# Tile loads and ScalarE copies moved ahead in the first two heads of a query, key, value stage

## The reference

```
def diff_attention(h, positions, w_qkv, lq1, lk1, lq2, lk2, subln_g, w_o, lambda_init):
    q, k, v = jnp.split(h @ w_qkv, 3, axis=-1)
    ...
    q = apply_rotary(q, cos, sin) * (HEAD_DIM ** -0.5)
    k = apply_rotary(k, cos, sin)
    ...
        s = jnp.einsum('bqhcd,bkhcd->bhcqk', q_blk, k, preferred_element_type=jnp.float32)
        p = jax.nn.softmax(s, axis=-1)
        a = p[:, :, 0] - lam * p[:, :, 1]
        return jnp.einsum('bhqk,bkhe->bqhe', a.astype(v.dtype), v)
```

## Time and profile before

| what | value |
|---|---|
| median of 3 runs | 2399.89 us (2398.41 to 2400.56) |
| the profiled execution, its own time | 2399.84 us |
| its span, first to last instruction | 2398.0 us |
| mean granted TensorE clock | 0.989 of 2.4 GHz |
| TensorE busy | 2311.8 us, 96% of the span |
| VectorE, ScalarE, GpSimd busy | 58%, 41%, 47% |

### The profile page before, as it was taken

One profiled execution on the slowest core, in us unless ns is written; L12 is line 12 of the kernel. 1 busy time (PEld: TensorE's weight loads), 2 busy tenths in 40 slices (PEclk: granted clock), 3 DMA queues, 4 the chain that ended last, 5 costly groups with the idle time before them and its releaser, 6 DMA issues.

```text
span 2398.0 us, 26048 instructions
## 1 busy us (share of the span) xinstructions
PE 2311.8 (96%) x10260; PEld 1884.2 (79%) x10260; DVE 1401.9 (58%) x1311; ACT 991.5 (41%) x1116; POOL 1138.8 (47%) x711
## 2 busy tenths in 40 slices
PE   8899989999999999999999999998999999999997
PEld 6688767777777888888888778887778888888886
DVE  7566799999375555556423654445565555563223
ACT  5112168888444444444312443233444444442112
POOL 1112113333467777775122677752776677732221
PEclk9999999999999999999999999999999999999998
DMA  3553374451322222322522322224222222234222
GB/s 130 170 175 120 132 201 114 97 135 36 124 93 80 79 79 80 93 84 99 200 91 90 108 71 74 75 88 175 80 88 82 86 79 79 83 128 176 90 80 93
DMA packets 79381, 254.23 MB, mean 106 GB/s; under 512 B 8608, under 2 KB 8992, under 8 KB 79264
## 3 DMA queue, kind: packets, MB, share of 16 engines
q1 hardware_dynamic: 79264, 252.63, 32.3%
HBM read 184.44 MB, written 68.16 MB: 105 GB/s over the span
## 4 chain that ended last, share of the span: by engine, by line
PE 72%; issue 14%; DVE 5%; POOL 5%; ACT 3%; DMA 1%; POOLq 0%; DVEq 0%; ACTq 0%
PE PS L306 24%; PE PS L830 14%; PE PS L831 14%; PE PS L832 14%; DVE nb L1393 2%; POOL Wst L291 2%; PE PS L749 1%; PE PS L727 1%; PE PS L735 1%; POOL X L1771 1%; PE PS L728 1%; DVE X L1412 1%; ACT X L1045 1%; DMA Wraw<-weights 1%; ACT X L1057 1%
## 5 line engine op out<-in xcount | busy, mean ns | idle before, releaser
L830 PE MATMUL PS<-XB,U 128*128 128x512 f32 x1532 | 599.8, 392 | 10.6 <-POOL U L1764 10.1
L832 PE MATMUL PS<-XB,U 128*128 128x512 f32 x1556 | 607.8, 391 | 0.0
L831 PE MATMUL PS<-XB,U 128*128 128x512 f32 x1532 | 598.6, 391 | 0.0
L291 POOL TENSOR_TENSOR Wst<-Wraw,Wst 128x1024 fp32r<-128x1024 f32 (+1 forms) x87 | 208.2, 2395 | 673.3 <-ACT Wst L285 673.3
L306 PE MATMUL PS<-H,Wst 128*128 128x512 f32 x2070 | 471.9, 390 | 2.5 <-POOL Wst L291 2.1
L306 PEld LDWEIGHTS PS<-H,Wst 128*128 128x128 f32 x2070 | 389.5, 188 | 84.6 <-POOL Wst L291 2.2
L830 PEld LDWEIGHTS PS<-XB,U 128*128 128x128 f32 x1532 | 289.3, 189 | 73.2 <-POOL U L1764 11.4
L832 PEld LDWEIGHTS PS<-XB,U 128*128 128x128 f32 x1556 | 293.7, 189 | 61.6
L831 PEld LDWEIGHTS PS<-XB,U 128*128 128x128 f32 x1532 | 289.5, 189 | 60.0
L1764 POOL TENSOR_TENSOR U<-U1f,U 128x2048 fp32r<-128x2048 f32 x56 | 259.5, 4635 | 8.6 <-ACT U L1125 1.0
L285 ACT ACTIVATE Wst<-Wraw 128x1024 fp32r<-128x1024 f32 (+1 forms) x87 | 88.4, 1020 | 380.0 <-DMA Wraw<-weights 379.8
(11 more groups left out here) (186 smaller groups left out, 3379.6 us busy)
## 6 DMA issues: line engine op xcount, KB each, us to landing
U1f<-ups SPq DMA_DIRECT2D x56, 512.0 KB, 4.5
U2f<-ups SPq DMA_DIRECT2D x56, 512.0 KB, 3.8
Wraw<-weights SPq DMA_DIRECT2D x55, 512.0 KB, 4.1
h_scratch<-Tv SPq DMA_DIRECT2D x47, 512.0 KB, 5.3
Hf<-h_scratch SPq DMA_DIRECT2D x44, 512.0 KB, 4.4
Wraw<-weights SPq DMA_DIRECT2D x32, 448.0 KB, 3.3
x_scratch<-X SPq DMA_DIRECT2D x24, 512.0 KB, 3.3
X<-x_scratch SPq DMA_DIRECT2D x24, 512.0 KB, 7.3
```

The costliest lines, as they stand in the source:

```text
L291: pool.tensor_tensor(w[:, 1, 0:cols], raw[:, 0:cols], w[:, 0, 0:cols].bitcast(F32), ALU.subtract).then_inc(w_lo, 1)
L830: pe.matmul(ps, wh, bh, start=begin, stop=False, skip_group_check=True)
L831: pe.matmul(ps, wh, bl, start=False, stop=False, skip_group_check=True)
L832: ins = pe.matmul(ps, wl, bh, start=False, stop=kp == KP - 1, skip_group_check=True)
```

## The change

SP issues the load of tile 5 ahead of the stores of head 0, the load of tile 6 between head 0's query and value stores, and the load of tile 8 ahead of head 1's key stores. ScalarE makes tile 4 ahead of head 0's `q_hi` and `v_hi`, and tile 5 ahead of head 0's `k_hi`. No instruction is added or removed.

```diff
-            for a in range(2):
-                qkv_head(a, a)
+            for n in (2, 3, 4, 5):
+                load_tile(sp, n, n % 2)
+            store_q(0)
+            load_tile(sp, 6, 0)
+            store_v(0)
+            store_k(0)
+            load_tile(sp, 7, 1)
+            store_q(1)
+            store_v(1)
             load_tile(sp, 8, 0)
+            store_k(1)
             sp.wait_ge(k_st, 32)
             load_k(0, 0)
             load_tile(sp, 9, 1)
...
                     h = pair * 2 + a
                     for j in range(3):
                         c = 3 * a + j
-                        if j == 2:
+                        if j == 2 and h:
                             q_hi(h)
                             v_hi(h)
-                        split_hi(act, pair * 3 + (c + 2) // 2, c % 2)
+                        if h != 1 or j:
+                            split_hi(act, pair * 3 + (c + 2) // 2, c % 2)
...
+                    if h == 0:
+                        q_hi(h)
+                        v_hi(h)
+                        split_hi(act, 2, 1)
                     k_hi(h)
```

## The result

Over six runs each the median is 2384.43 us (2380.62 to 2386.53) against 2399.16 (2398.03 to 2401.57) for the kernel before; the ratio is 0.993, with a 95% interval of 0.9919 to 0.994. The profiled execution took 2382.70 us with a span of 2380.9. The forecast was 2385.4, a gain of 14.4 us. The medians lie 14.7 us apart, and the interval of the ratio puts the gain at 14.4 to 19.4 us, its middle at 16.8. Direction and place were right, but the 1.6 us that were to come back as a wait did not. The times alone can't tell the forecast from its rival without that wait (2383.7 us), so the trace has to decide.

The account below looks back on a forecast made before the run. TensorE, busy 96% of the span, bounds the kernel, pausing for GpSimd's low parts of tiles 4, 5 and 8. Gain 16.2 - 1.6 - 0.15 = 14.4 us, so 2399.84 - 14.4 = 2385.4 us; range 2383.0 to 2388.5.

Parts of the forecast that it names:

- the 1.6 us that were to come back as a wait: Before tile 9: TensorE waits 1.6 us, its low part being ready at 115.4 and wanted at 113.8; bounds 0 and 2.4.
- rival without that wait: Nothing comes back before tile 9, its long landing shrinking: 2383.7 us, chance 0.25.
- The whole of what can be had: First to third transpose: 83.27 us against 67.10 for two steady heads, so pauses and slow starts are worth 16.17.
- Tile 4: Head 0: copied at 49.4, ready at 53.0, 4.7 us early; query's slot free at 57.0, 0.7 before need.
- the rival of the held rotation: GpSimd's part of tile 4 holds VectorE's rotation 2.4 us: gain 12.0, time 2387.8 us, chance 0.05.
- Tiles 5, 6 and 7: Loaded earlier by SP, ready at 65.1, 76.1 and 87.0 us for need at 68.6, 80.3 and 91.2.
- Tile 8: Head 1: ready at 98.6 to 103.4 us against need at 102.1; a wait of 0 to 1.3, taken as 0.
- VectorE's chain: Head 1: without rest once TensorE's pauses go, so its work ends and the value stores start at 91.0 us.
- the 0.15: Slower start after the wait before tile 9, costing 0.15 us.
- the same bytes stand in line afterwards: Value stores to tile 9's landing: the transfers again take 20.9 us, so tile 9 lands at 111.9.
- the rest of the program shifts as a block: Behind tile 9: everything is tied to TensorE's progress, so the rest only shifts.
- The clock: From 58 to 113 us: granted clock stays 1.00; rival of 1.2 GHz stretches gives 2405.4 us, chance 0.03.

Follow-up runs that it names:

- the first fix alone: Only ScalarE's new order for tile 4, against the kernel before the change: 2402.39 us against 2400.58, ratio 1.0009.
- the second alone: Only SP's new order of loads and stores, against the kernel before the change: 2392.51 us, ratio 0.9966.

## Why the prediction was right, and where it was wrong

- **The whole of what can be had, 16.17 us: right.** From first to third transpose the changed kernel takes 67.10 us, two steady heads to 0.01 us, where the earlier trace rows have 83.27.
- **Tile 4: right.** Its copy started at 49.42 (foretold 49.4), and neither `rot_read` nor GpSimd's part made it late. L1362 beside GpSimd (they overlap from 51.96 to 52.97) took 4.92 us, so the rival of the held rotation is out.
- **Tiles 5, 6 and 7: right.** No waits. Moving tile 6 back costs 1.7 us, about the 1.8 that its landing of 5.5 us gives.
- **Tile 8: right at 0.** It was ready at 100.8 for 102.1. That its move is worth 0.9 us and not 2.6 was seen only by moving it back.
- **VectorE's chain: right.** The value stores went out at 90.78 (foretold 91.0; the terms themselves add up to 90.9), and the query's rotation began at 72.02, at once behind `value_out`, as the chain without rest required.
- **"So 1.6 us come back": wrong, and with it the 0.15.** The failed step is "the same bytes stand in line afterwards, so tile 9 lands at 91.0 + 20.9". The line took 19.4 us and TensorE did not wait: tile 9 was ready at 113.69 and not at 115.4, 1.5 us of it by the line and 0.2 by VectorE's chain.

  Shown: 20.9 was one reading of something that came out as 20.1 and 20.4 in two more traces of the same kernel; with 20.1 or 20.4 in the sum, 0.8 or 1.1 us would have come back.

  Not settled: nine traces of kernels with the changed SP order, the key loads in place, gave 19.3 to 19.9, and four with the order of before 20.1 to 21.6, so a difference of 0.3 us or more looks real, and its cause stays open. It is not tile 8's place (19.6 with it behind). It is not tile 9 entering the line earlier, since in the kernel with SP's order alone it entered as late as before (12.5 us after the value store) and landed after 19.9. Nor is it how busy the transfers were (a DMA share of 0.98 over the line before, 0.99 after), nor, in the changed kernel, the queries: until tile 9 landed 5.81 MB moved before and 5.55 after, of which 5.24 are the line's own and the rest queries, but with none of them the line still took 19.8.

  The prediction's reading of the earlier trace rows was off too: that window runs 3.6 us past tile 9's landing, and from 117.2 to the landing the share was 1.03, at 242 GB/s and not 212.
- **Luck in the number.** The prediction gave this outcome, nothing coming back, 0.25 and 2383.7 us. The measured median, 2384.43, lies between that and the forecast, with runs that scatter over 6 us, so its nearness to 2385.4 says nothing for the term. The range was too narrow for such scatter: its own rule, half the spread of three runs under the best case, gives 2382.6 and not 2383.0, and a single run came at 2380.62. No wait came before tile 9, but that was close as well, since in the kernel with the queries behind a line of 19.8 us already cost 0.27 us.
- **The rest of the time.** In the two profiled executions, the 17.1 us between them are 16.2 in this stretch, 0.1 ahead of it, and 0.8 behind the third transpose (2398.0 - 129.18 = 2268.8 against 2380.9 - 112.90 = 2268.0). That last part scatters: 2264.4 in the second trace of the changed kernel, 2270.3 and 2269.7 in two of the kernel before. I took it as fixed ("the rest of the program shifts as a block").
- **The clock: right.** From 58 to 113 us TensorE was busy throughout and the granted clock was 1.00.

## What to carry to other kernels

Waits that stand in a row on one engine are not to be priced one by one: work out when each tile is ready by itself and take the latest. Here the first fix alone was worth nothing, the second alone 8 us, both 16. Where a forecast hangs on how long a crowded stretch of transfers takes, one trace gives one draw, and a margin of half a microsecond is then open both ways.

## What the runs showed of the hardware

**A race of 0.07 us for SBUF access that is worth 2 to 3 us.** In the projection after the attention VectorE makes three sums (in the code, differences; L1465, L1466, L1468) of two SBUF tensors each, in four places, and in the second of them GpSimd starts a tile's low part at nearly the same time as the third sum. The changed kernel's first trace, VectorE, then GpSimd, which starts at 650.64, then TensorE:

```profile
650.11 0.69 DVE L1466 TENSOR_TENSOR XBf<-XBf 128x512 f32<-128x512 f32 x1
650.71 2.89 DVE L1468 TENSOR_TENSOR XBf<-XBf 128x512 f32<-128x512 f32 x1
...
650.64 2.41 POOL L291 TENSOR_TENSOR Wst<-Wraw,Wst 128x1024 fp32r<-128x1024 f32 x1 [1.23 <-ACT Wst L285]
...
670.46 0.70 PE L306 MATMUL PS<-Yh,Wst 128*128 128x512 f32 x2 [2.24 <-POOL Wst L291]
```

The same kernel's second trace, where the weight tile landed 0.17 us after ScalarE was free for it, so that GpSimd came later and had to wait:

```profile
649.64 0.68 DVE L1466 TENSOR_TENSOR XBf<-XBf 128x512 f32<-128x512 f32 x1
650.24 0.69 DVE L1468 TENSOR_TENSOR XBf<-XBf 128x512 f32<-128x512 f32 x1
...
649.16 1.06 ACT L285 ACTIVATE Wst<-Wraw 128x1024 fp32r<-128x1024 f32 x1 [0.17 <-DMA Wraw<-weights]
...
650.30 2.90 POOL L291 TENSOR_TENSOR Wst<-Wraw,Wst 128x1024 fp32r<-128x1024 f32 x1 [1.37 <-ACT Wst L285]
```

In the first, VectorE ended 0.55 us after GpSimd; the next matmuls waited 2.24 us for a weight tile, and the granted clock was 0.83 from 670 to 680 us, where the second had 1.00:

```profile
670.00:680.00 10.00, 9.54 (x35) 7.76 (x36) 9.30 (x3) 1.73 (x2) 10.00 (x4) 0.83 0.22 90
```

In seven of the fourteen traces GpSimd's record starts 0.05 to 0.20 us ahead of the third sum, and the sum takes 2.88 or 2.89 us. In the other seven GpSimd starts from 0.02 us ahead to 0.17 us behind; there the sum takes 0.69, and GpSimd 2.79 to 2.98 instead of its usual 2.40. The one with GpSimd 0.02 us ahead (the kernel that only moves tile 23 too) went VectorE's way, so the recorded starts don't decide a tie as near as that. The Trainium skill (SBUF — State Buffer, "SBUF: two separate sides") says the same of all but the near tie, an exclusive lock for the whole instruction that goes to the first comer; the 2.89 us agree. In none of three traces of the kernel before did VectorE win.

What it costs further on only the traces show. Where this sum is held, the third sum of the next place is held too (2.88 us), in all seven traces; in the other seven it takes 0.68. The waits and the low clock above come on top. From the third transpose to the end, the seven traces with the sum held take 2267.6 to 2270.6 us, on average 2269.2; the five with it free that still have the wait before tile 23 take 2264.4 to 2268.2, on average 2266.7. So it is about 2.5 us on average, with ranges that overlap, in a kernel whose medians one wants to tell apart to 5 us.

**A pause costs more than once.** With tile 4 alone moved, the pause of 13.94 us stretched first to third transpose by 1.9 us over the earlier trace rows in these two traces, although the tile that it waited for came only 0.6 us later (82.56 - 45.78 against 82.06 - 45.91). Tile 5 itself took 95.85 - 82.56 = 13.29 us where it took 12.31 after the shorter pause and 10.92 is steady, and the wait before tile 8 grew by 0.3 us. The granted clock accounts for tile 5: by the trace's record it was 0.50 until 84.90 in the kernel before, 2.84 us into the tile, and until 87.43 with tile 4 alone moved, 4.87 us into it. At half the clock half of that time is lost, 1.4 and 2.4 us, and that is what the tile took beyond 10.92.
